# The 63 expert places in an alternating order: places with a second piece between places of 128 rows

## The reference, cut to what matters

```
scores = sigmoid(x @ router_w)                      # 1024 tokens x 64 experts
gates  = the 8 best experts of each token (4 of 8 groups), weights normalised
y[token] += gate * ((silu(x @ Wg[e]) * (x @ Wu[e])) @ Wd[e])    # for each chosen expert e
```

## Time and profile before

| | |
|---|---|
| time, median of 3 runs | 2622.13 us (2617.12 to 2624.11) |
| the profiled execution, span | 2625.4 us |
| PE busy | 2519.5 us, 96% |
| POOL busy | 510.2 us, 19% |
| DMA, mean over the span | 146 GB/s |
| DMA in the place stage | 284 to 364 GB/s in its slices |
| places, first to last `gate_up` of a place | 1682.7 to 2564.7 us |

### The profile page before, as it was taken

One profiled execution on the slowest core, in us unless ns is written; L12 is line 12 of the kernel. 1 busy time (PEld: TensorE's weight loads), 2 busy tenths in 40 slices (PEclk: granted clock), 3 DMA queues, 4 the chain that ended last, 5 costly groups with the idle time before them and its releaser, 6 DMA issues. The chain is left out here.

```text
span 2625.4 us, 27939 instructions
## 1 busy us (share of the span) xinstructions
PE 2519.5 (96%) x11230; PEld 1555.6 (59%) x11230; DVE 856.1 (33%) x1539; ACT 460.9 (18%) x756; POOL 510.2 (19%) x454
## 2 busy tenths in 40 slices
PE   6999999999999999999999999999999999999992
PEld 3444554345899444444445544587777777788881
DVE  5001654655534433323323532211122222211115
ACT  1001223335453100100000110111112222111110
POOL 2000111101453000000001054022333333222221
PEclk9999999999999999999999999999999999999996
DMA  6101003100000310111130420499999999999984
GB/s 242 56 32 64 1 32 101 48 8 9 1 1 25 112 48 25 48 48 48 64 137 5 152 65 18 165 335 340 284 288 305 289 296 309 322 364 358 357 272 152
DMA packets 159182, 382.73 MB, mean 146 GB/s; under 512 B 14384, under 2 KB 34608, under 8 KB 158288
## 3 DMA queue, kind: packets, MB, share of 16 engines
q1 hardware_dynamic: 133200, 294.25, 31.5%
q0 software_dynamic: 24848, 79.68, 12.1%
q10 hardware_dynamic: 1008, 7.02, 0.7%
HBM read 320.14 MB, written 60.78 MB: 145 GB/s over the span
## 5 line engine op out<-in xcount | busy, mean ns | idle before, releaser
L1799 PEld LDWEIGHTS banks<-arena 128*128 128x128 f32 x4096 | 520.7, 191 | 45.3 <-issue 42.9
L1799 PE MATMUL banks<-arena 128*128 128x128 f32 (+7 forms) x4096 | 529.7, 290 | 2.7 <-DVE arena L2175 2.0
L1354 PE MATMUL banks<-arena 128*128 128x512 f32 x672 | 293.2, 597 | 1.3 <-PEq L710 1.3
L307 PE MATMUL banks<-arena 128*128 128x512 f32 x640 | 280.9, 596 | 4.7 <-DVE arena L1067 4.3
L2219 POOL DMA_INDIRECT acc_scratch<-arena x99 | 153.0, 1545 | 607.2 <-DMA acc_scratch<-arena 349.1
L1807 PE MATMUL banks<-arena 128*128 128x512 f32 (+1 forms) x528 | 242.5, 602 | 1.6 <-DVE arena L2178 0.9
L1354 PEld LDWEIGHTS banks<-arena 128*128 128x128 f32 x672 | 128.4, 191 | 163.9 <-issue 163.7
L307 PEld LDWEIGHTS banks<-arena 128*128 128x128 f32 x640 | 120.2, 190 | 159.2 <-issue 149.5
L300 PE MATMUL banks<-arena 128*128 128x512 f32 x384 | 168.7, 597 | 0.6 <-PE banks L300 0.6
L1383 PE MATMUL banks<-arena 128*128 128x512 f32 x384 | 166.7, 592 | 0.0
L2156 DVE TENSOR_TENSOR arena<-arena,banks 128x256 f32<-128x256 f32 (+7 forms) x63 | 29.1, 462 | 421.9 <-PE banks L1799 416.9
(11 more groups left out here) (356 smaller groups left out, 2580.7 us busy)
## 6 DMA issues: line engine op xcount, KB each, us to landing
arena<-in_exp_w_gu SPq DMA_DIRECT2D x64, 2048.0 KB
arena<-in_exp_w_down SPq DMA_DIRECT2D x64, 1024.0 KB, 12.4
arena<-in_w_in SPq DMA_DIRECT2D x10, 2048.0 KB, 9.1
arena<-in_w_in SPq DMA_DIRECT2D x12, 1024.0 KB
arena<-in_w_branch SPq DMA_DIRECT2D x12, 512.0 KB
arena<-in_x SPq DMA_DIRECT2D x4, 1024.0 KB, 14.9
h_scratch<-arena SPq DMA_DIRECT2D x1, 4096.0 KB, 11.1
arena<-in_w_out SPq DMA_DIRECT2D x2, 2048.0 KB, 7.9
```

Source lines behind the costliest of these rows:

```text
L307: last = nc.tensor.matmul(PS[:, bank, :], wt[:, k, ct * P:(ct + 1) * P], hT[:, k, half * HALF:(half + 1) * HALF], start=(k == 0), stop=(k ...
L1354: last = nc.tensor.matmul(PS[:, g % 4, :], lhs[:, k, :], rhs[:, k, :], start=(k == 0), stop=(k == 3))
L1799: last = nc.tensor.matmul(PS[:, bank + part, f * n:(f + 1) * n], weights[:, k, part * FF + f * P:part * FF + (f + 1) * P], by_k(x, n)[:, k ...
```

## The change

```diff
+def place_order():
+
+    double = [r for r in range(NE - 1) if rank_rows(r) > P]
+    single = [r for r in range(NE - 1) if rank_rows(r) == P]
+    at = {r: i / len(double) for i, r in enumerate(double)}
+    at.update({r: (i + 1) / len(single) for i, r in enumerate(single)})
+    return sorted(range(NE - 1), key=lambda r: (at[r], r)) + [NE - 1]
+
+PLACES = place_order()
+
+def place_rows(q):
+
+    return rank_rows(PLACES[q])
...
-    put("ranks", np.broadcast_to(np.arange(NE), (P, NE)))
-    put("caps", np.broadcast_to([rank_rows(r) for r in range(NE)], (P, NE)))
+    put("ranks", np.broadcast_to(PLACES, (P, NE)))
+    put("caps", np.broadcast_to([place_rows(q) for q in range(NE)], (P, NE)))
...
         def more(r):
-            return rank_rows(r) - P
+            return place_rows(r) - P
...
+        def seconds(r):
+
+            return 16 * sum(more(q) > 0 for q in range(r % 2, r + 1, 2))
...
                 def more_rows_in(r):
                     c = chunks(r)
-                    pe.wait_ge(x_inB[r % 2], 16 * (r // 2) + 16)
+                    pe.wait_ge(x_inB[r % 2], seconds(r))
...
-                        gather(xgA[r % 2], 2 * q, P, x_inA[r % 2])
+                        gather(xgA[r % 2], 2 * PLACES[q], P, x_inA[r % 2])
                         if more(q):
-                            gather(xgB[r % 2], 2 * q + 1, more(q), x_inB[r % 2])
+                            gather(xgB[r % 2], 2 * PLACES[q] + 1, more(q), x_inB[r % 2])
...
-                    add_rows(yoA[r % 2], 2 * r, P)
+                    add_rows(yoA[r % 2], 2 * PLACES[r], P)
...
-                        add_rows(yoB[r % 2], 2 * r + 1, more(r))
+                        add_rows(yoB[r % 2], 2 * PLACES[r] + 1, more(r))
```

More of the change, by code:

```diff
@@ L1846, in _ @@
                 for r in range(NS):
-                    n, c = rank_rows(r), chunks(r)
+                    n, c = place_rows(r), chunks(r)
                     pe.wait_ge(x_wg[r % RING], 16 * (r // RING) + 16)
@@ L1920, in x_half @@
                 def x_half(r, lo, n):
-                    nc.scalar.activation(by_k(xT[r % 2], rank_rows(r))[:, 0:4, lo:lo + n], bank4(0, n), ACT.Copy).then_inc(x_xa, 1)
+                    nc.scalar.activation(by_k(xT[r % 2], place_rows(r))[:, 0:4, lo:lo + n], bank4(0, n), ACT.Copy).then_inc(x_xa, 1)
                 def y_half(r, out, gate, n, c, bank):
@@ L1938, in _ @@
                 for r in range(NS):
-                    n, c, c1 = rank_rows(r), chunks(r), chunks(r + 1)
+                    n, c, c1 = place_rows(r), chunks(r), chunks(r + 1)
                     act.wait_ge(x_g, r + 1)
@@ L2114, in x_half @@
                 def x_half(r, lo, n):
-                    nc.vector.tensor_copy(by_k(xT[r % 2], rank_rows(r))[:, 4:8, lo:lo + n], bank4(1, n)).then_inc(x_xv, 1)
+                    nc.vector.tensor_copy(by_k(xT[r % 2], place_rows(r))[:, 4:8, lo:lo + n], bank4(1, n)).then_inc(x_xv, 1)
                 def y_half(r, out, gate, n, c, bank):
@@ L2141, in gates_in @@
                     if more(r):
-                        v.wait_ge(x_inB[r % 2], 16 * (r // 2) + 16)
+                        v.wait_ge(x_inB[r % 2], seconds(r))
                         nc.vector.tensor_scalar(gateB[r % 2][0:more(r), :], xgB[r % 2][0:more(r), bass.ds(e + D, 1)], 1.0, None,
@@ L2225, in _ @@
                 pool.wait_ge(f_int, 1)
[L2226 to L2229, removed]
+                for q in range(2):
+                    gather(xgA[q], 2 * PLACES[q], P, x_inA[q])
+                    if more(q):
+                        gather(xgB[q], 2 * PLACES[q] + 1, more(q), x_inB[q])
                 for r in range(NS):
```

## The result

The changed kernel takes 2641.89 us (median of 4 runs, 2638.57 to 2643.60) against 2620.53 us (4 runs, 2617.12 to 2624.11) on the same chip: ratio 1.0072, interval 1.0047 to 1.0098. It is 21 us slower where 5 were forecast, and outside the stated range. The profiled execution has a span of 2641.8 us and is the slowest of the four: a run's time is 1.8 us more than its span here (2643.60 us). The same 1.8 us belong on the span of the profiled execution of before. With 2627.2 us it lay 5.1 us over the median of its three runs and 3.1 over the slowest, not 3.3 and 1.3 as stated ahead of the prediction.

What follows compares the result with a forecast made beforehand. PE, busy 96%, was taken as the bound, with loss in smaller double places through late gathers. Terms -16.2 + 17.7 + 2.5 = +4.0 us gave 2629.4 (profiled) or 2626.1 (median); forecast 2627.5 us, eight-in-ten range 2613 to 2638.

Steps and rivals of the forecast that it cites:

- (b), the cover of piece B's copies: PE's gate_up of a double place behind a single one waits for DVE's copy: 26 changes, 17.7 us, bounds 13 to 23.
- (a), the waits that go: PE's waits for gathers in the place stage, with restarts and lower-clock stretches, hold 16.2 us; most of the waiting must go.
- (a), the waits that stay: PE's remaining gather waits, mainly where two double places stand together: 2.5 us kept, between 0 and 10.
- The add's price: POOL's chain of adds takes 14.8 us for a double place and about 9.9 for a single one, 24.7 per pair.
- The clock: PE's granted clock does not fall under 26 short gate_up waits, 0 us; the opposing rival had 44 us, chance 0.03.
- The weights: PE needs place 8's expert weights about 15 us earlier, yet never waits for weights: 0 us taken.
- The sum: Whole kernel: -16.2 + 17.7 + 2.5 = +4.0 us against the profiled execution's 2625.4, giving 2629.4.
- My second rival: Double places outrun POOL's adds where two stand together, so rows_in waits: +15 us, 2637 us; chance 0.29 with milder cases.

Runs made afterwards that it cites:

- exposed copies: Kernel before, old order, with PE's down projection of piece B moved ahead of the next piece B's transposition: 2639.2 us against 2622.1, ratio 1.0059.
- The old order with early gathers: Kernel before, with POOL issuing a later place's gathers between the adds of piece A and piece B: 2623.3 us against 2620.5, ratio 0.9994.

## Why the prediction was wrong, point by point

- **(b), the cover of piece B's copies: right in mechanism, too small.** The waits are there at 26 places and their sum is the predicted 17.7 us. The whole effect is 23.6 us, 0.9 per change, just over my upper bound of 23: this term is short by 5.9 us. The 0.2 us over the wait is lost where unlike places meet, and it is there without any wait too (25.59 against 25.39 us above). `gate_up` of a single place behind a double one takes 7.41 us instead of 7.30, and the transposition of a piece B starts 3.53 us after piece A's down projection (2357.45 to 2360.98), where the next `gate_up` of the old order's single places starts after 3.44. The old trace had this once, at its only change from double to single. I had read the wait's price and not compared whole places.
- **(a), the waits that go: the profiled execution was taken for the usual one.** I gave the waits 16.2 us; by the medians leaving out the second adds gains 11.8, by the two profiled spans (2625.4 and 2607.4) 18.0. So the reading of that execution was sound, and it was a slow one. I saw that it lay over the median, though by 5.1 us and not by the 3.3 that I read, and took half the difference.
- **(a), the waits that stay: this step failed.** I gave 2.5 us, from a pace: 24.7 us of adds for a pair against 26.0 of PE. The runs show 8.0 us, of two kinds. At the five waits behind couples the pace was wrong: I carried the old order's turn, from one place's add A to the next's, of 14.8 us, at worst 16.1, into the new one, and it was 16.6 us there (mean of 22 turns from 1975 us on, 14.7 over 18 turns in the old order). PE spends only 13.3 us on a double place in front of a single one, so a couple pushes the next add A back by 2.4 to 3.6 us, where I had 0.9 to 2.2. At the other four the adds were in time, and what I had left out decides, the way of one result: landing of add A 9.7 us, add B, the gather 9.6, together 21, against the length of the next place and one `gate_up`. A single place behind a double one makes this window shorter, 21.0 instead of 13.93 + 8.11 = 22.0 us. Both kinds go when the gather no longer stands behind the landing of add A. The old trace had shown them together at its first two single places (waits of 1.0 and 2.5 us, add A some 4 us late), right in front of the second window of the earlier trace rows, which I read for the clock alone.
- **The add's price.** For the single place I took 9.9 us from one wait of ACT that a landing may have ended only just. In the new order POOL waited for a single place's add only once from 1975 us on, and that one had landed after 8.9 us: with 16.6 + 8.9 us a pair stays within PE's 26.3, and this is why the turns of mere alternation cost nothing. While add A of a double place was under way, from 1745 us on, the queues moved 253 GB/s on average in the old order and 305 in the new, and the add took 8.4 us in the one and 9.8 in the other. The Trainium skill (DMA: Bandwidth & Descriptors, Latency and other measured facts) says that lighter HBM load makes the fixed cost of a DMA smaller; the trace agrees in direction, and the 6.2 us of gather waits are nearer 5 than 0, as I had written under that rule. Whether the traffic is the cause was not tried: in the new order add A also starts right with its result in most places, beside other weights and gathers than before.
- **The clock** did not swing under 26 waits of 0.6 to 0.8 us, as I held. Behind longer waits it fell in some cases and not in others. It fell behind 2.32 and 2.54 us in the old order. With exposed copies it did not behind 2.80 us. Behind the wait of 2.0 us at the spill block, which every version has, it fell in two of the fourteen profiles. **The weights** were never waited for.
- **The sum.** Forecast +4.0 against the profiled execution; the pieces as measured against medians are -11.8, +23.6 and +8.0. The 4.4, 5.9 and 5.5 us between them and my terms explain the miss. My second rival had the right place, the couples, and its condition, a turn of about 16 us, was met; but it had 10 us of waits and 3.8 us of clock and restarts where 8.0 us came in all, and it left the 5.9 us of (b) out. That its 2637 us lie near the measured time is in part luck.

## What to carry to other kernels

Before reordering loop bodies of two kinds, list what each kind hides for its neighbour: a filler that exists only in the longer body is gone at every change of kind, and here that cost more than the balance gained. Judge an in-order queue with dependent DMAs by both its pace and the latency of one item through it; a mean can have room while each item comes late. And an independent transfer should not be queued behind a dependent one: moving the gathers between the two adds made the mixed order free of gather waits and 9 us faster. In the order of 36 double places in a row the same move gained nothing in the median.

## What the runs showed of the hardware that I had not expected

- An accumulating DMA of 128 rows of 4 KB to HBM, between weight loads and gathers, took 8.4 us from its issue to the next issue in the old order and 9.8 in the new (means over 30 and 29 double places, 6.4 to 11.4 each), at 253 and 305 GB/s while it ran. A gather of 128 rows issued behind one was there for PE after 9.6 us.
- PE takes 0.1 us more for a first run of 128-column matmuls behind the down projection of a second piece (7.41 instead of 7.30 us for 64), and a small transposition or down projection follows a run of 512-column matmuls 0.1 us later than a `gate_up` does (3.53 against 3.44 us). Together this is 0.2 us per change of kind, and invisible as a wait.
- The length of a wait alone did not tell whether the granted clock fell behind it: a wait of 2.80 us was followed by no fall, and one of 2.0 us, the same in all fourteen profiles, by a fall of 3.4 us at 1.2 GHz in two of them.
- The old order with early gathers had runs from 2610 to 2636 us with all instructions the same, and the kernel before beside it runs from 2616 to 2649. Without second adds, four runs lie within 1.5 us. So the scatter comes with the chain of adds; that a queue which is a few us behind makes it is my reading, not shown by a run.
